# Local attention woven into the recurrence's first block, and memory attention begun ahead of the last query slot

## The reference

```python
for l in range(DEPTH_2):                       # 2 layers
    x = x + 0.5 * swiglu(rms_norm(x, norm_ffn1[l]), ffn1_wi[l], ffn1_wo[l])
    h = rms_norm(x, norm_mix[l])
    p = h @ w_in[l]
    p_a, p_q, p_k, p_v, p_c = jnp.split(p, split_pts, axis=-1)
    y_a, v_first = rwkv7_mixer(p_a, v_first, ...)      # recurrence, 6 heads of 64
    y_b = chunk_attention(p_q, p_k, p_v, ...)          # local attention, 6 heads of 64
    y_c = multiscale_pool(p_c, ...)                    # 4 groups of 64 channels
    x = x + jnp.concatenate([y_a, y_b, y_c], axis=-1) @ w_out[l]
    x = x + memory_cross_attention(rms_norm(x, norm_cross[l]), rms_norm(mem, norm_mem[l]), ...)
    x = x + 0.5 * swiglu(rms_norm(x, norm_ffn2[l]), ffn2_wi[l], ffn2_wo[l])

def step(S, inp):                              # the recurrence, per token and head
    sa = jnp.einsum('bhvk,bhk->bhv', S, -kk_t)
    S = (S * w_t[:, :, None, :] + sa[..., None] * (kk_t * a_t)[:, :, None, :]
         + v_t[..., None] * k_t[:, :, None, :])
    return S, jnp.einsum('bhvk,bhk->bhv', S, r_t)
```

## Time and profile before

| what | us |
|---|---|
| median of 3 executions | 2627.58 (2620.62 to 2631.18) |
| the profiled execution | 2626.4 |
| its span, first to last instruction | 2624.6 |
| TensorE busy in the span | 2305.2 |
| VectorE busy | 1069.0 |
| ScalarE busy | 857.3 |

### The profile page before, as it was taken

The page is one execution under the profiler, slowest core; times in us unless marked ns, Lnnn a source line. Parts: engine busy times, 40 slices in busy tenths (PEclk is TensorE's granted clock), DMA queues, the critical chain, the costliest instruction groups (busy, mean ns, idle before and its releaser), DMA issues.

```text
span 2624.6 us, 37287 instructions
## 1 busy us (share of the span) xinstructions
PE 2305.2 (88%) x15288; PEld 1641.8 (63%) x15288; DVE 1069.0 (41%) x1681; ACT 857.3 (33%) x1348; POOL 77.0 (3%) x87
## 2 busy tenths in 40 slices
PE   7998998677787777776779999899999999899999
PEld 7996593233333333222238888788888889778887
DVE  7767761000000000000025467565555547555544
ACT  4483140000010000000034455355445445445543
POOL 0000012000000000000000001000000000200000
PEclk9999999888887888889889999999999999899999
DMA  6434089999999999999986543144556554023553
GB/s 244 173 135 144 2 337 392 427 427 427 427 427 427 427 426 427 427 427 427 427 339 216 192 166 115 35 161 136 186 192 202 191 192 153 33 99 117 187 190 115
DMA packets 116818, 669.15 MB, mean 255 GB/s; under 512 B 10826, under 2 KB 14069, under 8 KB 56400
## 3 DMA queue, kind: packets, MB, share of 16 engines
q1 hardware_dynamic: 111376, 650.14, 63.7%
q0 software_dynamic: 3008, 12.96, 1.4%
q10 hardware_dynamic: 2304, 4.20, 0.4%
HBM read 662.01 MB, written 5.24 MB: 254 GB/s over the span
## 4 chain that ended last, share of the span: by engine, by line
PE 56%; DMA 25%; SPq 5%; DVE 5%; issue 3%; ACT 2%; DVEq 2%; POOLq 1%; ACTq 0%; POOL 0%
PE psd L641 22%; PE psd L635 10%; PE psx L641 9%; DMA scr<-in_w_up 8%; DMA ring<-in_w_down 7%; DMA hx<-in_w_down 6%; SPq L3032 5%; DMA e_w_hi<-in_w_up 2%; PE psd L1044 1%; DVE scr L2083 1%; PE psx L1059 1%; PE psd L1006 1%; PE psx L1300 1%; DMA ring<-in_w_gate 1%; PE psx L885 1%
## 5 line engine op out<-in xcount | busy, mean ns | idle before, releaser
L2083 DVE TENSOR_TENSOR w_lo<-ring,w_hi 128x1024 fp32r<-128x1024 f32 x436 | 515.8, 1221 | 392.2 <-ACT w_hi L1543 391.3
L1543 ACT ACTIVATE w_hi<-ring 128x1024 fp32r<-128x1024 f32 x436 | 437.0, 1048 | 474.8 <-PE psd L641 248.7
L641 PE MATMUL psd<-w_hi,h_cut 128*128 128x512 f32 x1536 | 481.4, 395 | 3.9 <-DVE h_cut L2083 3.5
L635 PE MATMUL psd<-h_cut,w_hi 128*128 128x256 f32 x1824 | 337.3, 287 | 12.1 <-DVE h_cut L2083 7.8
L641 PEld LDWEIGHTS psd<-w_hi,h_cut 128*128 128x128 f32 x1536 | 284.2, 188 | 61.5 <-DVE h_cut L2083 4.4
L641 PE MATMUL psd<-w_lo,h_cut 128*128 128x512 f32 x768 | 300.2, 391 | 0.0
L635 PEld LDWEIGHTS psd<-h_cut,w_hi 128*128 128x128 f32 x1824 | 288.0, 194 | 16.6 <-issue 13.9
L635 PE MATMUL psd<-h_cut,w_lo 128*128 128x256 f32 x912 | 260.1, 285 | 0.0
L641 PE MATMUL psx<-w_hi,halves 128*128 128x512 f32 x704 | 218.0, 391 | 0.0
L1532 ACT ACTIVATE scr<-psd 128x512 f32<-128x512 f32 x48 | 28.6, 596 | 566.3 <-PE psd L1022 359.4
L2083 DVE TENSOR_TENSOR scr<-psd,scr 128x512 f32<-128x512 f32 x20 | 13.8, 690 | 435.4 <-PE psd L1006 435.3
(11 more groups left out here) (391 smaller groups left out, 2901.0 us busy)
## 6 DMA issues: line engine op xcount, KB each, us to landing
ring<-in_ffn_wi SPq DMA_DIRECT2D x88, 1024.0 KB, 5.3
scr<-in_w_gate SPq DMA_DIRECT2D x48, 1024.0 KB, 26.6
scr<-in_w_down SPq DMA_DIRECT2D x48, 1024.0 KB, 26.2
scr<-in_w_up SPq DMA_DIRECT2D x48, 1024.0 KB, 26.9
ring<-in_ffn_wo SPq DMA_DIRECT2D x44, 1024.0 KB, 4.9
ring<-in_w_gate SPq DMA_DIRECT2D x32, 1024.0 KB, 26.6
ring<-in_w_up SPq DMA_DIRECT2D x32, 1024.0 KB, 27.0
ring<-in_w_down SPq DMA_DIRECT2D x32, 1024.0 KB, 26.5
```

The costliest lines, as they stand in the source:

```text
L635: mm = pe.matmul(o, w[u], a[:, v, :], start=start and i == 0, stop=stop and i == 2, **kw)
L641: mm = pe.matmul(o, a[:, u, :], w[v], start=start and i == 0, stop=stop and i == 2)
L1543: act.activation(hi, src, ACT.Copy).then_inc(hi_cut, 1)
L2083: return dve.tensor_tensor(o, a, b, op)
```

## The change

Two things are rewritten. In the second block, the local attention no longer stands ahead of the recurrence: its heads are placed between the steps of block tt = 0, with its results in `psd` banks. And the memory attention's heads 0 to 2 are started inside and ahead of the last query slot; head 3 gets its own norm bank and its own root.

Place of the results in the `psd` ring:

```diff
+def attention_banks(early):
+    if early:
+        return [("av_tr", 0, "act"), ("av_tr", 1, "act"), ("score", 0, "dve"), ("score", 1, "dve"), ("score", 2, "dve"),
+                ("prob_tr", 0, "act"), ("score", 3, "dve"), ("prob_tr", 1, "act"), ("score", 4, "dve"),
+                ("prob_tr", 2, "act"), ("score", 5, "dve"), ("prob_tr", 3, "act")]
+    return [("prob_tr", 4, "act"), ("prob_tr", 5, "act"), ("att", 0, "act"), ("att", 1, "act"), ("att", 2, "act"),
+            ("pool", 0, "act"), ("att_share", 0, "dve"), ("att_share", 1, "dve")]
```

TensorE's stream, block 0 (lines with + are new at this place):

```diff
+                turned(0, "ab")
+                score(0)
                     pair("A", al, be)
                     pair("AT", be, al)
+                        score(1)
+                        turned(0, "kv")
                     mats("P2", ...)
                     mats("P2T", ...)
                     pair("BT", kt, al)
+                        score(2)
                     mats("Q2", ...)
                     mats("P4", ...)
                     mats("P4T", ...)
+                        prob_back(0)
+                        score(3)
                     pair("CT", be, rt, P)
                     mats("Q4", ...)
                     mats("P8", ...)
+                        prob_back(1)
                     pair("DT", kt, rt, P)
+                        score(4)
                     mats("Q8", ...)
                     mats("TR", ...)
                     mats("X1", ...)
+                        prob_back(2)
+                        score(5)
                     mats("BV", ...)
                     mats("Q32", ...)
-                        (the bonus matmuls)
+                        prob_back(3)
                     mats("WU", ...)
                     ...
                         for g, name in ((1, "b"), (2, "k"), (3, "v")):
                             turned(1, name)
                             state_step(g)
+                            if g < 3:
+                                prob_back(3 + g)
+                        for q in range(HP):
+                            attended(q)
+                        pooled()
+                        shares()
+                        (the bonus matmuls)
                         b = from_chunks()
```

VectorE's stream, block 0: `kt` and `rt` are scaled right behind the last projection. Then:

```diff
                     keys_turned(0); masked A, AT; q_begun
+                        scored(0)
                     masked(tt, "BT"); add_to_q(tt, "Q2")
+                        scored(1)
                     masked(tt, "CT", P)
-                        (bonus_in)
                     add_to_q(tt, "Q4")
+                        scored(2)
                     masked(tt, "DT", P); add_to_q(tt, "Q8")
-                        (wait mix_rest_hi, low part of the rest)
+                        scored(3)
+                        scored(4)
                     add_to_q(tt, "Q32")
-                        bonus()
+                        scored(5)
+                        (bonus_in)
                     (M, R)
+                        dve.wait_ge(S("pooled"), l + 1)
+                        state(0)
+                        shares_spread()
+                        for g in range(1, 4):
+                            state(g)
+                        keys_turned(1)
+                        attention_scaled()
+                        bonus()
                         bonus_gated()
+                        dve.wait_ge(S("mix_rest_hi"), l + 1)
+                        tt_(h_lo[:, 3:8, :], ycat[:, 3:8, :], h_hi[:, 3:8, :].bitcast(F32),
+                            ALU.subtract).then_inc(S("mix_rest"), 1)
```

ScalarE's stream, block 0:

```diff
+                solved(0, "P2", "P2T")
+                score_exp(0)
+                solved(0, "P4", "P4T")
+                prob_kept(0)
+                score_exp(1)
+                solved(0, "P8")
+                prob_kept(1)
+                score_exp(2)
+                solved(0, "TR", "X1")
+                prob_kept(2)
+                solved(0, "BV")
+                score_exp(3)
+                prob_kept(3)
+                solved(0, "WU")
+                turned(1, "a")
+                score_exp(4)
+                score_exp(5)
+                turned(1, "k")
+                prob_kept(4)
+                turned(1, "v")
+                prob_kept(5)
+                attention_kept()
+                cutter.upto(slot_of((("mix_out", l), 0)))
+                from_chunks(0)
+                cutter.upto(slot_of((("mix_out", l), 1)))
```

The memory attention on TensorE, VectorE and ScalarE:

```diff
+                dense((("x_q", l), 2), mn_cut)                     # TensorE
+                x_norm(b, 0)
+                x_norm(b, 1)
+                pe.wait_ge(S(f"kv_in{l}"), 80)
+                x_score(0)
+                dense((("x_q", l), 3), mn_cut, middle=third_head)  # x_norm 2, x_score(1), x_score(2)
+                x_prob_back(0)
+                x_score(3)
+                x_norm(b, 3).then_inc(S("x_normed"), 1)
+                x_prob_back(1)
+                x_prob_back(2)
+                x_attended(0)
+                x_attended(1)
+                x_prob_back(3)
+                x_attended(2)
+                x_attended(3)
...
+                x_top(0)                                           # VectorE, behind x_query and cut_ahead of 0 to 2
+                x_scales(slice(0, 6), 0)
+                x_max(0)
+                x_top(1); x_max(1); x_top(2); x_max(2)
+                divide(0)
+                x_query(3)
+                x_top(3)
+                divide(1)
+                divide(2)
+                cut_ahead(cutter, (("x_q", l), 3))
+                x_scales(slice(6, 8), 1)
+                x_max(3)
                 divide(3)
...
+                act.activation(r16[:, 0:6], ..., ACT.Sqrt, ...)    # ScalarE, behind x_square(0) to (2)
+                x_exp(0)
+                x_exp(1)
+                x_exp(2)
+                cut_ahead(cutter, (("x_q", l), 3))
+                x_square(3)
+                x_prob_kept(0)
+                act.activation(r16[:, 6:8], ..., ACT.Sqrt, ...)
+                x_exp(3)
+                for hd in range(1, 4):
+                    x_prob_kept(hd)
```

More of the change, by code:

```diff
@@ L303, in small_plan @@
                 add("act", "vup", l, i)
-        add("act", "av_tr", l, 0)
-        add("act", "av_tr", l, 1)
-        for step in range(8):
-            if step < 6:
-                add("dve", "score", l, step)
-            if step > 1:
-                add("act", "prob_tr", l, step - 2)
-        for q in range(HP):
-            add("act", "att", l, q)
-        add("act", "pool", l)
-        for tt in range(TT):
-            add("dve", "att_share", l, tt)
         def turned(tt, names):
@@ L338, in small_plan @@
                 turned(1, "bkv")
+                for i in range(2):
+                    add("dve", "bonus", l, 0, i)
             add("act", "Y", l, tt)
@@ L344, in small_plan @@
         add("act", "xnorm", l, "q", 0)
-        for h in range(4):
+        for h in range(3):
             add("act", "xscore", l, h)
-        for h in range(4):
+        add("act", "xprob_tr", l, 0)
+        add("act", "xnorm", l, "q", 1)
+        add("act", "xscore", l, 3)
+        for h in (1, 2):
             add("act", "xprob_tr", l, h)
-        for h in range(4):
+        for h in (0, 1):
+            add("dve", "xatt", l, h)
+        add("act", "xprob_tr", l, 3)
+        for h in (2, 3):
             add("dve", "xatt", l, h)
@@ L456, in x_ready, with a_ready @@
             return XB.bank(key)
+        ATTENTION = {}
+        for l in range(LAYERS):
+            for early in (True, False):
+                for part, i, _ in attention_banks(early):
+                    ATTENTION[part, l, i] = len(ATTENTION) + 1
+        def a_ready(eng, *key):
+            eng.wait_ge(S("attention_done"), ATTENTION[key])
+            return DB.bank(key)
         PAIRS = pair_order()
@@ L1350, in _ @@
                     if tt == 0:
-                        pe.wait_ge(S("rk_ready"), l + 1)
-                        for i in range(2):
-                            b = m2(XB.claim(pe, ("bonus", l, 0, i)))
-                            for m in range(2 if i == 0 else 1):
-                                mm = pe.matmul(b[:, m, :], bones, bonus_in[:, 2 * i + m, :], start=True, stop=True)
-                            done(mm)
+                        prob_back(3)
                     mats("WU", "Q", lambda p, q: ab[:, 2 * q + p, :], n=P, wait=after("Q32", "BV"))
@@ L1418, in _ @@
                             state_step(g)
+                            if g < 3:
+                                prob_back(3 + g)
+                        for q in range(HP):
+                            attended(q)
+                        pooled()
+                        shares()
+                        pe.wait_ge(S("rk_ready"), l + 1)
+                        for i in range(2):
+                            b = m2(XB.claim(pe, ("bonus", l, 0, i)))
+                            for m in range(2 if i == 0 else 1):
+                                mm = pe.matmul(b[:, m, :], bones, bonus_in[:, 2 * i + m, :], start=True, stop=True)
```

(9 more changed lines are left out.)

366 lines of the change are left out of this document (206 added, 160 removed).

## The result

| what | before | after |
|---|---|---|
| median, us | 2625.9 (2620.62 to 2631.18, 4 runs) | 2604.36 (2603.85 to 2605.45, 4 runs) |
| profiled execution / its span | 2626.4 / 2624.6 | 2603.85 / 2602.0 |
| TensorE, VectorE, ScalarE busy | 2305.2, 1069.0, 857.3 | 2300.4, 1070.8, 860.8 |

A forecast was written before the change was run, and what follows sets the result against it. Chains of short handoffs laid end to end, attention then recurrence, were taken to bound the changed stretch. 2626.4 - 18 (attention) + 2 (memory attention) = 2610.4, plus 1.2 for the median: 2611.5 us, range 2602 to 2623.

The forecast's parts named there:

- Start, 19.3 earlier: Local attention, second block: block 0's masks of A begin 19.3 us earlier per layer, at about 2258.65 instead of 2277.97.
- The sentence that POOL's two results cost nothing: Woven stretch: POOL's mixed and pooled values start as before and are needed later relative to it, so they cost nothing.
- WU, 3.05 later: Block 0, masks of A to WU: inserted heads delay VectorE's masks and additions, making WU 3.05 us late.
- Tail, 6.7 longer: WU to block 1's masks of A: added TensorE work 5.4, state steps 1.0, late VectorE 0.3; 6.7 us longer.
- One layer, 9.6, doubled to 18: Woven attention: 19.3 - 3.05 - 6.7 = 9.6 us gained in layer 1, taken as 9, doubled to 18.
- the allowance of 0.6: Woven attention: one layer's 9.6 us gain lowered to 9 for a handoff or two estimated too short.
- The clock, 1.00 throughout: Sign for the woven stretch: TensorE's granted clock near 1.00 throughout, with 128x128 transposes at 272 ns.
- Rival D: Woven block: TensorE granted the lower clock; change loses from 9 us of issue on, 2654 at two thirds; chance 0.06.
- Memory attention, +2: Query slot 2 to projection: 30.0 us by head 3's chain, plus 0.5 a layer for the clock; together +2 us.
- The rule on tiling modes: Transposes between 64x64 groups: a mode change drains TensorE; wholly on the path, 2 us a layer, gain 7, not 9.
- B: Rival: in-order VectorE and ScalarE queues eat the woven attention's gain; one layer gains 3.2, total 2623; chance 0.27.
- C: Rival: memory attention gains too, 4.2 us a layer, if divisions and splits slip into waits; total 2601; chance 0.12.

The follow-up runs named there:

- e6_pool_waits: The changed kernel, with POOL's last addition into the values and its pooling waiting until VectorE has scaled kt and rt; 2603.74 us (one run).
- e7_wu_first: The changed kernel, with the fourth turned head and its copy behind WU instead of ahead of it; 2601.44 us (one run).
- e5_rest_late: The changed kernel, with VectorE's low half of the mix moved from the end of block 0 to behind block 1's first low split; 2601.17 us (one run).
- e3_busy: The kernel before, with matmuls whose result nobody reads put into TensorE's waits of the local attention; 2622.49 us (10 runs), ratio 0.9993.
- e1_att_only: The changed kernel with the memory attention of the kernel before, so only the local attention is woven; 2604.84 us (4 runs), ratio 0.993.
- the two pairs: Before/after profiles of both kernels: the first profiles, and a second profile of each, unchanged; net gain of the attention stretches 19.9 and 20.5 us.
- e4_splits_late: The changed kernel, with the memory attention's splits moved behind head 3's chain and the two divisions ahead of its maximum; 2599.27 us (4 runs), ratio 0.9904.

## Why the prediction was right, step by step

**Start, 19.3 earlier.** 18.8 in layer 1 and 19.8 in layer 0. Right on average, by chance, since I worked it out for layer 1, where it is 0.5 too much: kt and rt were priced at 2 x 0.95 from a row in which POOL's addition did not run beside them, and took 3.44. That cost 0.75 there, and 0.5 more ahead of WU (e6_pool_waits). The sentence that POOL's two results cost nothing was the one that failed: as work they were hidden, as a neighbour they were not.

**WU, 3.05 later.** 2.7 in both layers. The masks and additions slipped as written, and 0.67 of it is the turned head 3 ahead of WU (e7_wu_first); the 0.71 us wait for ScalarE ahead of 2264.92 is the one that I named.

**Tail, 6.7 longer.** 6.3 in layer 1. Of the kernel before, R and the first outputs Y in layer 1, and the stall inside R in layer 0:

```profile
2299.52 0.88 PE L1394 MATMUL psx<-scr 128*64 128x128 f32 x12
...
2303.87 0.44 PE L1406 MATMUL psx<-scr 128*64 128x128 f32 x4
...
1671.57 0.43 PE L1394 MATMUL psx<-scr 128*64 128x128 f32 x2 [0.82 <-issue]
```

By its parts, from the timelines: states 0.54 more (R to the next product 4.35 before, 2274.87 - 2269.98 = 4.89 after; I took 1.0); products, pool, shares and bonus 2280.00 - 2274.87 = 5.13 (I took 5.4); Y to the masks 2284.54 - 2280.00 = 4.54 against 3.93, 0.61 more (I took 0.3). VectorE was later than I had it, 1.4 or more behind the moment the masks could begin (e5_rest_late), not 0.3: the key copy, which ended the wait there before (L2813 in the earlier trace rows), now comes earlier, so the masks could have begun sooner than they did before. The two errors nearly cancel.

**One layer, 9.6, doubled to 18.** Layer 1 gave 9.75; layer 0 gave 12.10. The steps held, each within 0.5, and the allowance of 0.6 was not needed. The term that was mis-sized is layer 0, which I took as equal because two of its stretches are as long. Its tail was 14.19, not 12.88, with the 0.82 us stall inside R, which the earlier trace rows are not from and so cannot show. From R's start to the transposes behind it took 2.05 us there and 0.81 in layer 1. The woven kernel has no stall there: 1.3. The start gives 1.0 more (0.24 longer before, 0.75 shorter after). These make 2.35 of the 3.85 us by which the attention beat 18; the other 1.5 is twice the 0.75 between 9.75 and the 9 that I took. One reading in the forecast's signs was off: its 51.7 for the whole stretch ends at TensorE's A product (2307.17 in the earlier trace rows); to the masks, as the sum has it, it is 52.31. With 9.6 less that gives 42.7, and layer 1 measured 42.56.

**The clock, 1.00 throughout.** It held in the four stretches of the changed kernel's two profiles, and the 128x128 transposes in the first profile have a median of 273 ns (272 forecast). In layer 1 it was lost right behind the stretch, both times, for 1.1 us, which the forecast did not have. It was worth about 3 us a layer of the attention stage (e3_busy). Rival D was a real mechanism at a small size: 4.3 us at 0.60 cost 1.5 in layer 1 in two of the variants, far from the 9 us at which the change would lose.

**Memory attention, +2.** +1.94 and +3.17 in the two pairs. Slot 3 ended 13.6 us behind query 2 (13.8 forecast). Head 1's product began 10.5 behind slot 3's end in both layers (10.3), ended by ScalarE's copy as written, so the chain was right. What followed depends on the clock. In layer 0 the wait was 2.73 (2.6), but head 1's product ran at half rate and the projection began 17.6 behind slot 3's end; in layer 1 the wait was 1.29 and the projection began at 16.1 (16.2). The wait of the forecast and its 16.2 were met in different layers, and the 0.5 a layer that I added for the clock was in fact some 1.5 in one layer of two. That the sum comes to 2 is in part luck. In all four stretches of the changed kernel one product is at half rate. Where it is head 0's, the wait behind it hides it, and the stretch takes 29.65; where it is head 1's, 31.1. The kernel before took 28.77 three times and 30.14 once, at a granted clock of 0.94 and 0.89 (e1_att_only, with the same memory part, has the same pair: 28.80 and 30.44). So the cost is 0.9 a layer, and 1.4 to 1.55 more by where the lower level falls; the -0.49 of layer 1 compares a bad stretch of before with a good one of after, and is no gain. I blamed the wait ahead of head 1 for the lower level; in layer 1 the half-rate product stands ahead of that wait, so it is not what brings it. The two table loads took 1.28 each and hid, as forecast: ScalarE idled 2.60 us behind them. By the 2.66 us a switch of the Trainium skill (ScalarE: Activation LUTs, What ACT_TABLE_LOAD costs), an estimate has the second end at 2379.95, 0.1 behind the exponential's start; the trace does not agree with that price.

**The rule on tiling modes** (TensorEngine Tiling (Array Packing), Tiling Modes, Key Properties). A turned head put between two state steps, beside the transposes that stood there before, lengthens the step from 1.03 to 1.30 us; no other group of the new order was priced by itself. By the Trainium skill's drain, wholly on the path, the forecast's estimate was a gain of 7 for the layer. It gave 9.75, so that worst case is not seen.

**Rivals.** B is out: of VectorE's 9.4 us for six heads 2.7 show up to WU. C did not happen in this order, and e4_splits_late shows why: its mechanism was there (26.37, 2.4 below even the best stretch of before), and the two divisions and two low splits (2.36 us) that the written order put ahead of head 3's scale held it back. D came at a small size only.

**Open.** What the 0.82 and 1.37 us stalls labelled issue are; they stand at one place of the program, and no wait of another engine is seen to end them. There are others: every profile here of either kernel and its variants but e3_busy has one of 0.5 to 1.1 us at a state step of layer 1's block 1. Why the clock is lost at some starts of the woven stretch and not at others, and in some executions right behind it instead: the row ahead of the loss (3.98 of 5.00 us busy) and that of the changed kernel (4.17 of 5.20) are alike. And 1 to 1.6 us of the median's gain (21.5, against 19.9 and 20.5 in the profiles), which is within the spread of the kernel before.

## What to carry to other kernels

Two chains of short handoffs laid end to end are worth weaving when each leaves the other's engines idle: walk the new order handoff by handoff with the old durations, and work out every copy of the stage, since equal order is not equal time. Work put ahead of schedule is worth only as much as the chain behind it on each engine: before starting heads early, ask which in-order queue holds the last head, and move the bulk work (here two splits) behind it and short work into its waits (here two divisions). An unrelated engine's elementwise work can be a cost if it lands beside one that is on the path, as POOL's addition did here.

## What was not expected of the hardware

- VectorE's two 128x768 operations took 3.44 us beside POOL's 128x768 addition (0.95 and 2.58) and 1.82 with POOL held back; POOL's took 2.62 and 1.81. The operations and their shapes are the same; only the neighbour differs.
- Keeping TensorE at work through the attention's waits raised the granted clock from 0.66 and 0.74 to 0.91 and 1.00, but in layer 0 the lower level came later instead (0.74). The kernel's gain of 2 us (-1.3 to 5.0 by its interval) cannot be told from nothing.
- A TensorE stall of 0.8 to 1.4 us stands at one place of a program in two executions, and not at the same matmuls in the other layer; six matmuls more ahead of it moved the place (e3_busy).
- One kernel can be granted 1.00 in one execution and 0.59 for 4 us at the same place in another (block 1 of layer 1, kernel before). Each such loss here cost 1.1 to 1.5 us, so a difference of that size between two profiles needs a third before it is given a cause.
